# Decoder trunk with product-key experts on one core: front end for pairs of blocks, vector adds in the dense rows

## The reference

```python
h = rmsnorm(x, norm_mix);   x = x + hybrid_mixer(h)            # w_in -> MLA 4 heads | RG-LRU 512 | differential attention 4 heads -> w_out
h = rmsnorm(x, norm_cross); x = x + cross_attention(h, mem)    # 256 memory rows, 4 heads; w_cq, w_ckv, w_co
h = rmsnorm(x, norm_ffn);   x = x + peer_ffn(h)
out = rmsnorm(x, norm_final)

def peer_ffn(h, w_q, keys, u, v):                              # per token and head (8 heads)
    sc = q @ keys (2 x 128);  top16 of each;  top16 of the 256 sums -> experts, best_s
    act = gelu(einsum('td,thkd->thk', xt, u[et]));  return einsum('thk,thkd->td', softmax(best_s) * act, v[et])
```

## Time and profile before

| | us |
|---|---|
| three executions | 3482.92, 3485.80, 3488.39 |
| profiled execution | 3488.4, its span 3488.4 |
| first u gather issued | 277.5 |
| first and last row product (L2052) | 306.6, 3461.8 |
| PE, DVE, POOL, ACT busy | 2948.9, 2349.6, 2015.7, 812.5 |
| moved | 1345 MB, of which 1073.87 MB expert rows |

### The profile page before, as it was taken

One profiled execution on the slowest core, in us unless ns is written; L12 is line 12 of the kernel. 1 busy time (PEld: TensorE's weight loads), 2 busy tenths in 40 slices (PEclk: granted clock), 3 DMA queues, 4 the chain that ended last, 5 costly groups with the idle time before them and its releaser, 6 DMA issues.

```text
span 3488.4 us, 34790 instructions
## 1 busy us (share of the span) xinstructions
PE 2948.9 (85%) x10984; PEld 1651.9 (47%) x10984; DVE 2349.6 (67%) x5893; ACT 812.5 (23%) x1915; POOL 2015.7 (58%) x2085
## 2 busy tenths in 40 slices
PE   7876898888988898889997899888998889976675
PEld 6465455544545355534554456444564445522222
DVE  6229846886588765886578765886648865596555
ACT  3111411132211421133211322114221232211111
POOL 1004755666566765666565655665556655477775
PEclk9898999999999999999999999998999999999998
DMA  7788999999999999999999999999999999999998
GB/s 279 277 274 313 408 409 409 408 409 409 409 407 406 394 409 409 408 407 382 409 409 408 392 356 409 409 409 348 359 409 409 409 355 342 385 404 410 409 409 347
DMA packets 386971, 1345.09 MB, mean 386 GB/s; under 512 B 41762, under 2 KB 44834, under 8 KB 386148
## 3 DMA queue, kind: packets, MB, share of 16 engines
q0 software_dynamic: 294912, 1073.87, 78.1%
q1 hardware_dynamic: 90724, 264.79, 20.0%
q10 hardware_dynamic: 1152, 4.19, 0.3%
HBM read 1332.99 MB, written 35.39 MB: 392 GB/s over the span
## 4 chain that ended last, share of the span: by engine, by line
PE 38%; DMA 30%; DVE 15%; POOL 9%; issue 6%; ACT 3%; SPq 1%; DVEq 0%; POOLq 0%; ACTq 0%
PE ps_sum L1267 18%; DMA rows<-in_peer_u,ids_u 13%; DMA rows<-in_peer_v,ids_v 10%; PE ps_p L999 5%; POOL rows L824 5%; POOL rows L810 4%; DVE rows L2052 4%; PE ps_s L1181 4%; DMA rows<-in_peer_v,ids_u 3%; DMA w_ring<-packed 3%; PE ps_s L1118 2%; PE ps_p L1126 2%; DVE feat_b L1935 1%; DVE feat_b L1931 1%; PE ps_s L1114 1%
## 5 line engine op out<-in xcount | busy, mean ns | idle before, releaser
L1267 PE MATMUL ps_sum<-rows,diag 128*128 128x512 f32 x3548 | 1727.6, 629 | 267.1 <-DMA rows<-in_peer_v,ids_v 141.4
L2052 DVE CUSTOM_DVE_ANT_0 rows<-h_cur,rows 128x1024 f32<-128x1024 f32 x1024 | 1226.8, 1220 | 496.3 <-DMA rows<-in_peer_u,ids_u 483.3
L810 POOL DMA_INDIRECT rows<-in_peer_u,ids_u x1024 | 1012.3, 989 | 702.0 <-issue 483.3
L1267 PEld LDWEIGHTS ps_sum<-rows,diag 128*128 128x128 f32 x3548 | 671.0, 200 | 1155.7 <-issue 1005.7
L824 POOL DMA_INDIRECT rows<-in_peer_v,ids_v x512 | 490.3, 958 | 433.8 <-PE ps_sum L1267 277.6
L824 POOL DMA_INDIRECT rows<-in_peer_v,ids_u x512 | 498.2, 973 | 284.7 <-PE ps_sum L1267 144.2
L1528 ACT ACTIVATE diag<-ident,acts 128x128 f32<-128x128 f32 x887 | 324.7, 394 | 1049.4 <-PE ps_sum L1267 750.1
L999 PE MATMUL ps_p<-hT,w_ring 128*128 128x128 f32 x2944 | 358.7, 282 | 28.8 <-DMA w_ring<-packed 15.3
L999 PEld LDWEIGHTS ps_p<-hT,w_ring 128*128 128x128 f32 x2944 | 353.0, 198 | 61.2 <-issue 39.7
L1834 DVE CUSTOM_DVE_ANT_0 e<-ps_s,bias_t 128x256 f32<-128x256 f32 (+6 forms) x96 | 74.2, 773 | 176.3 <-PE ps_s L1118 73.7
L2074 DVE SCALAR_TENSOR_TENSOR x_cur<-rows,acts,x_cur 128x1024 f32<-128x1024 f32 x137 | 175.6, 1282 | 7.4 <-DMA rows<-in_peer_v,ids_v 7.3
(11 more groups left out here) (288 smaller groups left out, 2376.2 us busy)
## 6 DMA issues: line engine op xcount, KB each, us to landing
w_ring<-packed SPq DMA_DIRECT2D x343, 512.0 KB
w_ring<-in_wstream SPq DMA_DIRECT2D x65, 512.0 KB
packed<-in_wstream SPq DMA_DIRECT2D x49, 512.0 KB, 8.2
rows<-in_peer_u,ids_u POOLq DMA_INDIRECT x1024, 14.9
rows<-in_peer_v,ids_u POOLq DMA_INDIRECT x512, 12.6
rows<-in_peer_v,ids_v POOLq DMA_INDIRECT x512, 19.3
bias_rows<-rows SPq DMA_DIRECT2D x5, 1024.0 KB, 12.1
bias_t<-in_x SPq DMA_DIRECT2D x8, 512.0 KB, 7.9
```

What stands on the lines that cost most here:

```text
L810: pool.indirect_dma_start(u_rows[:, slot, :], None, peer_u, bass.IndirectOffsetOnAxis(ap=ids_u[:, j:j + 1], axis=0)).then_inc(u_landed[slo ...
L1267: ins = pe.matmul(ps_sum[:, c * 512:(c + 1) * 512], diag[:, n % 4, :], v_rows[:, slot, c * 512:(c + 1) * 512], start=(j == 0), stop=(n == ...
L2052: dve.tensor_tensor_reduce(row, h_cur[:, :], row, 1.0, 0.0, ALU.mult, ALU.add, dots[:, p:p + 1]).then_inc(u_used, 1)
```

## The change

The front end now works on a pair of blocks c (256 tokens; `NC` = 4), and a weight tile is loaded once for the pair: 16 + 4 x 49 = 212 loads in place of 16 + 8 x 49 = 408, and the 49 copies of `pack` are gone. All weight loads read the array with the 2 KB runs. `w_ring` has 3 slots, the two rings 8 each. `project` and `queries` stream 256 columns against a stationary weight tile; `row_product` streams each weight half twice, for the two token blocks, into four PSUM banks. Latents, heads, recurrence and join stay per block. `next_at`, `pair_at`, `attention_at`, `top_at` in place of the tables give the row of the pair's 256 at which a stage stands: attention of block 2c at 44 to 96 and of 2c+1 at 96 to 148, dense stages 148 to 216, choice of block 2c at 217 to 254, choice of 2c+1 at 256 to 293, which is in the rows of the next pair, and the projection of the pair after at 224 to 272. Before row 0 lies the whole front end of pair 0, except the second block's choice; the memory's 32 pieces stand in the heads of the blocks 0 and 1 (`beside`), 16 in each.

The loops of single blocks are gone: all rows 0 to 1023 are written out, with constant waits. In the rows in which the dense stages run DVE adds three v rows in four, 263 in all where it was 137. For the last pair that rule does not hold. PE spreads the experts' gain into `h_cur` at each block's start, which waits for the last product of the block before (`u_used`), and the final gain into `ps_sum` after the square; the first sum of the next block waits until the output is scaled (`fin_made`). The residual `x` of the pair after is loaded again by a DMA of ACT's queue into `x_next[P, 2, D]`.

```diff
-W_RING = 4
-U_RING = 9
-V_RING = 9
+NC = NB // 2
+PAIR = 2 * EXPERTS
+ROWS = NB * EXPERTS
+W_RING = 3
+U_RING = 8
+V_RING = 8
...
-def on_vector(b, j):
-    return j % SHARE == SHARE - 1 or (b == NB - 1 and j >= TAIL and j % 2)
+ATTENTION_AT, ATTENTION = 44, 52
+TOP_AT, SECOND_TOP_AT, TOP = 217, 256, 37
+DENSE_FROM, DENSE_TO = 146, 214
+def adds_on_vector(q):
+    j, at = q % EXPERTS, (q + SUM_LAG) % PAIR
+    if q >= ROWS - 24 and j % 2 == 1:
+        return True
+    if DENSE_FROM <= at < DENSE_TO and q < ROWS - PAIR:
+        return j % 4 != 0
+    return j % SHARE == SHARE - 1
...
+            def project(c):
...
+                        w = weight(weight_number(c, tile)).rearrange("p (k c) -> p k c", k=KT)
...
+                            dst = p_bank[k % 2][:, i * 2 * P:(i + 1) * 2 * P].rearrange("p (s t) -> p s t", s=2)
+                            for kt in range(KT):
+                                ins = pe.matmul(dst, w[:, kt, :], h_pair[:, :, kt, :], start=(kt == 0), stop=(kt == KT - 1))
...
+            def row_product(c, first, norm, row):
...
+                        w = weight(weight_number(c, first + 4 * n + j)).rearrange("p (k c) -> p k c", k=2)
+                        for half in range(2):
+                            kt = 2 * j + half
+                            for s in range(2):
+                                ins = pe.matmul(four_banks[2 * n + s], h_of[s][:, kt, :], w[:, half, :], start=(kt == 0), stop=(kt == KT - 1))
+                        ins.then_inc(w_used, 1)
```

More of the change, by code:

```diff
@@ L259 @@
[L259 to L270 removed]
+STEP = 8
+STEPS = EXPERTS // STEP
 GATE_LAG = 1
@@ L762, in _ @@
[L762 to L770 removed]
+                             rope_d[:, :, b * P:(b + 1) * P].rearrange("c r t -> r c t")).then_inc(rope_landed, 16)
@@ L1294, in _ @@
-            for pace.body, (first, last, wide[0]) in enumerate(LOOPS):
-                if first == 2:
-                    front["mla_up"] = later_up
-                if first == NB - 1:
-                    front["peer_scores"] = last_scores
-                with pe.Fori(first, last) as b:
-                    pace.start(b - 1)
-                    pace.run(stages(front, last=first == NB - 1), b)
-            pace.start(NB - 1)
-            pace.to(SUM_LAG - 1)
-            pe.wait_ge(handed, NB)
@@ L1457, in diff @@
+                pace.to(attention_at(b, first))
                 exp_scores(b, 4 + 2 * h, e0)
[L1458 removed]
+                beside(b, 8 + 2 * h)
+                pace.to(attention_at(b, second))
                 exp_scores(b, 5 + 2 * h, e1)
[L1460 removed]
+                pace.to(attention_at(b, turn))
                 out_pT(b, 4 + h)
[L1463 to L1467 removed]
@@ L1561, in _, with position @@
-            front["latents"] = project_3
-            for pace.body, (first, last, wide[0]) in enumerate(LOOPS):
-                with act.Fori(first, last) as b:
-                    pace.start(b - 1)
-                    pace.run(stages(front, last=first == NB - 1), b)
-            pace.start(NB - 1)
+            def position(p):
+                b, j = divmod(p, EXPERTS)
+                if p % STEP == STEP - 1 and p < ROWS:
+                    act.wait_ge(u_used, U_RING + p + 1)
+                    act.activation(acts[:, j - STEP + 1:j + 1], dots[:, j - STEP + 1:j + 1], ACT.Gelu).then_inc(acts_made, 1)
+                if b and j == SQUARE_AT:
+                    square_out(b - 1)
+                if b and j == STORE_AT:
+                    store_out(b - 1)
+                if j == HAND_AT + 1 and b + 2 < NB:
+                    act.wait_ge(x_handed, b + 1)
+                    act.dma_start(x_next[:, b % 2, :], x[(b + 2) * P:(b + 3) * P, :]).then_inc(res_landed[b % 2], 16)
+                q = p - DIAG_LAG
+                if q < 0 or q >= ROWS or ON_VECTOR[q]:
+                    return
+                n = sums_before(q)
+                act.wait_ge(coef_made, q // STEP + 1)
+                act.wait_ge(v_used, n + SUM_SLOTS - 3)
+                at = q % EXPERTS
+                act.activation(diag[:, n % 4, :], ident[:, :], ACT.Copy, scale=coef[:, at:at + 1]).then_inc(diag_made, 1)
```

1662 lines of the change are left out of this document (780 added, 882 removed), and 36 rows, old and new, of tables (SCALAR_STOPS, VECTOR_STOPS).

## The result

The changed kernel takes 3534.6 us (median of four runs, 3528.7 to 3537.9), the kernel before 3484.4 beside it: a ratio of 1.0148, 95% interval 1.0132 to 1.0164. I had forecast 3476, a gain of 0.3%: the time lies inside my range of 3420 to 3550, and the sign is the other one. The profiled execution has a span of 3535.7 us, 47.3 more than before.

The account below looks back on a forecast made before the run. The row phase was taken as bound by DMA transfers at 409 GB/s. From 3488.4 us, -234 transfers, +182 start and +42 idle DMA time gave 3478.4 profiled, 3476 as median, a gain of 0.3%; range 3420 to 3550.

Parts of the forecast that it names:

- What bounds the kernel: Row phase: bound by DMA transfers at a ceiling of 409 GB/s, 97% of the time.
- term 1: Transfers in the row phase: fewer weight tile loads, now in 2 KB runs, save 234 us (207 to 243).
- the upper price: Weight tiles in 2 KB runs: upper bound of 1.54 us a tile, where 1.34 was taken.
- Term 2, the start: Before the first gather: the front end of two blocks stands before row 0, +182 us (+165 to +215).
- my third rival: Start: the clock falls in the two attentions, making the start longer by 30 us, 3506; chance 0.15.
- Term 3: Idle DMA time in the row phase: grows from 96 to 138 us, +42 (bounds -10 and +120).
- PE also now waits at a block's end for the square and DVE's scale before the first sum, some 5 us; two of these fall into its bound stretch, +5: Block switches: PE's new waits before the first sum add 5 us of idle DMA time.
- Rings of 8 and not 9 ... I take 3: Row rings: one slot less in each costs 3 us, between 0 and above 30.
- The late part, PE-bound for wide blocks, keeps its work and loses two rows: Late attention heads, 52 rows a block and not 56: 98 -> 94 us against 69 us of transfers.
- Vector adds: Dense rows: DVE's extra adds take PE from 267 to 184 us a pair, making the shared tiles usable.
- Doubled choice: Rows 217 to 293, two expert choices in succession: DVE 233 us against DMA 225, +18 us of idle time.
- the rival that ended on the right side: Doubled choice of experts: DVE becomes the bound, idle DMA time grows 85 us, 3521; chance 0.25.

Follow-up runs that it names:

- e11: Kernel after with weights laid out in DRAM so that a tile is read in 4 KB runs, not 2 KB: 3523.4 us, 11.2 faster.
- e2: Kernel after without PE's two gain spreads at a block switch and their waits, both gains left out of the computation: 3494.0 us, 40.6 faster.
- e9: Kernel before with 8 slots in each of the two row rings, not 9: 3501.6 us against 3484.0, ratio 1.0060.
- e10: Kernel after with attention 56 rows a block from row 36, not 52 from row 44: 3590.3 us, 55.7 slower.
- e13: Kernel after with attention at rows 40 to 152, 56 rows a block, both blocks starting at a multiple of eight: 3523.6 us.
- e4: Kernel after with every second v row added on DVE in rows 70 to 96 and 118 to 141 too: 3577.6 us, 43.0 slower.
- e8: As e4, but the additions beyond one in eight are left out and DVE only frees the slot: 3553.6 us, 19.0 slower than the kernel after.
- e12: Kernel before with every second v row on DVE in rows 28 to 56 of blocks 1 to 6: 3505.8 us against 3484.0, ratio 1.0058.
- e16: Kernel after with the edits of e13, e11 and e2 together: 3480.4 us, ratio 0.9994 to the kernel before.
- e3: Kernel after with one v row in eight on DVE in the dense rows too, not three in four: 3603.0 us, 68.4 slower.

## Why the prediction was wrong

- *What bounds the kernel, and term 1*: right. 409 GB/s is the ceiling after as well (405 beside tiles of 2 KB runs), 212 tiles and 1220 MB came as told, and the transfers fell by 233 with the price of these runs (forecast 234). 2 KB runs cost what I took: by the packets 5% a byte, 1.34 us a tile. e11 gave 11 us back where the term holds 8, and the upper price, 1.54 us a tile, would have been 36. The Trainium skill's price ("DMA: Bandwidth & Descriptors", "Why small descriptors are slow (HBM only)"), 2.3% a tile, would be an estimated 4 us and is too low by these packets.
- *Term 2, the start*: right to 1 us at the first gather (182.5), and by steps: the projection fills 63.6 of the 64 us from 16 to 80, the shared products 133 of 141. A 256-column record takes 217.1/960 = 0.226 us, so the cost goes by columns and two blocks on one weight load save PE nothing. The Trainium skill's cheaper column in a longer stream ("TensorE: Matmul & The Clock Gate", "Back-to-back issue gap") does not show in this kernel after the change either. The clock did fall in both attentions (0.56 in 80 to 119, 0.62 in 179 to 239), without the price of my third rival. PE was busy 16.6 of 39 and 34.3 of 60 us there, so the chain may simply not notice; no run tests it. First gather to first product took 6 us longer than before; by e2 that is the first spread and its waits, which this term did not have.
- *Term 3*: this failed, +91.5 in place of +42. "PE also now waits at a block's end for the square and DVE's scale before the first sum, some 5 us; two of these fall into its bound stretch, +5" was the step: the spreads and their waits cost 41 us in all (e2). It is two spreads a block, each a synchronisation of PE with DVE. In the 5 us behind each of the eight spreads of the final gain the granted clock is 0.50; behind those of `h_cur` it is 0.54 to 0.66 in six of eight and 1.00 in two. The kernel before has spreads too, and no run takes them out there; its switches lose under 1 us of DMA time, so I count its share as nothing.
- "Rings of 8 and not 9 ... I take 3": 17.6 us by e9. I argued from one rate (POOL can't win back) and not from the many short stalls that a slot covers.
- "The late part, PE-bound for wide blocks, keeps its work and loses two rows": wrong in kind. The late heads lost 129 us in the kernel after (99 and 30), where I had 85 + 5 for the whole attention. PE's busy time in the heads is only in part an amount of work. With the same work it grew and shrank with the phase of the steps (e10, e13), and with less work it hardly shrank (e4, e8, e12). The kernel after is 11 us slower than e13, where 54 us less in the heads stand against 43 more in the dense rows.
- These three are 41 - 5, 17.6 - 3 and 11, 62 us together where they don't overlap, and the error was 57 in the profiled execution (3535.7 against 3478.4). That the sums are near each other proves little: the 17.6 were measured in the kernel before, the 11 are a net figure inside the noise, and in e16 spreads, phase and 4 KB runs give 54 us together for a sum of 63.
- *Vector adds*: the sign was right and the size not, 68 us for 150 (e3). Of the 25 us a pair that are missing, the too dear row sum makes about 7 and the too large rest of PE's work (151 us for 131) about 20.
- *Doubled choice*: 18 us forecast, though 24 - 8 is 16. Rows 217 to 293 took 244 us in the first pair (129.5 and 114.2), 11 more than my 233, and 216.5 in the last, 16.5 less; the idle time there is 37 us in all where I had 26. PE, not DVE, was the late one in 224 to 256: busy 102 of 104 us, with DVE at 84. So the rival that ended on the right side gave the wrong reason; its 3521 was near by accident. Its 85 us don't follow from its own prices either: 29 + 29 + 50 and 16 for the attention, less the 8 of before, are 116.

## What to carry to other kernels

A stretch with a busy engine is only bound by that engine's amount of work if its clock stays where it is; before moving work off a PE that also waits on a chain, read the granted clock of the window, and ask which engine will release the slots afterwards. Halving weight traffic by pairing blocks pays bytes with start time and with buffer slots, and both must be priced: here 235 us of transfers saved were paid for with 189 us of start, some 18 of ring, and the waits of a hand-over that no longer had a slack place to stand. A synchronisation moved into a tight stretch costs more than its own length: 16 spreads of 1.8 us at full clock cost 41 us with their waits. Where stages of one engine are interleaved with batches of another, try the same order shifted by half a batch before changing anything else.

## What the runs showed of the hardware

- Taking 34 to 42 PE instructions out of a window of heads left its busy time within 5% for block 6 of the changed kernel (79.0, 78.4 and 75.2 us), as the granted clock fell from 0.89 to 0.73 and 0.75. In the kernel before it fell from 90.8 to 84.2 us for block 5 (clock 0.95 to 0.83) and rose from 100.4 to 103.9 for block 7 (0.95 to 0.77).
- A shift of four rows in the order of the same instructions changed the granted clock of a window from 0.85 to 0.98 and the kernel by 66.7 us.
- Reading weights in runs of 2 KB in place of 4 KB lowered the rate of a mixed stretch from 409 to 405 GB/s at the same share of 1.03; a 2 KB packet took 86.0 ns, a 4 KB one 163.9.
- A spread of 1024 columns (four records) took 0.59 us a record in the kernel before, and 1.06 us a record at the median for the final gain in the kernel after, where the granted clock was 0.50.
